# Attention: the first head pair begins its units after two groups' maxima, and takes the other groups' maxima inside its units

## The reference

```
s = einsum('bqhd,bkhd->bhqk', q_blk, k_all)
s = s + fq_blk.transpose(0, 2, 1)[..., None] - f_k[:, :, None, :]     # F = running sum of log forget values
s = where(kpos <= qpos, s, -inf)
p = softmax(s, axis=-1)
o = einsum('bhqk,bkhd->bqhd', p, v_all)
```

## Time and profile before

| | us |
|---|---|
| median of 3 runs | 3133.67 |
| the 3 runs | 3128.68, 3133.67, 3133.70 |
| the profiled execution | 3129.55 |
| its span, first to last instruction | 3128.0 |
| its mean granted PE clock | 0.945 of 2.4 GHz |
| attention: PE's first transpose to the first unit | 2004.04 to 2044.02 |
| attention: the 8 pairs' units | 2044.02 to about 2850 |

### The profile page before, as it was taken

One profiled execution on the slowest core, in us unless ns is written; L12 is line 12 of the kernel. 1 busy time (PEld: TensorE's weight loads), 2 busy tenths in 40 slices (PEclk: granted clock), 3 DMA queues, 4 the chain that ended last, 5 costly groups with the idle time before them and its releaser, 6 DMA issues. The chain is left out here.

```text
span 3128.0 us, 41449 instructions
## 1 busy us (share of the span) xinstructions
PE 2843.9 (91%) x15730; PEld 2033.8 (65%) x15730; DVE 1476.7 (47%) x3562; ACT 945.1 (30%) x1547; POOL 804.0 (26%) x460
## 2 busy tenths in 40 slices
PE   5589999997899996999969999789999999994999
PEld 2367777776677874788758777455555555552767
DVE  1542222211787646641157015566666666653343
ACT  0322222211555654220033112134444444433000
POOL 1220000000000002000011000268887888786000
PEclk7589999999899998999989999789999999997999
DMA  9532222212566435211151331333313431313764
GB/s 337 196 89 81 54 85 81 78 48 87 178 209 218 155 98 200 78 59 67 49 177 48 78 72 50 101 109 100 88 57 106 116 93 37 112 34 134 245 204 133
DMA packets 281927, 355.20 MB, mean 114 GB/s; under 512 B 40044, under 2 KB 172460, under 8 KB 281681
## 3 DMA queue, kind: packets, MB, share of 16 engines
q1 hardware_dynamic: 279364, 344.23, 34.9%
q0 software_dynamic: 2304, 8.39, 0.7%
q10 hardware_dynamic: 72, 0.07, 0.0%
HBM read 250.28 MB, written 102.10 MB: 113 GB/s over the span
## 5 line engine op out<-in xcount | busy, mean ns | idle before, releaser
L2341 POOL TENSOR_TENSOR at_p_sum<-at_p_sum,at_p 128x1024 f32<-128x1024 f32 (+3 forms) x264 | 521.9, 1977 | 84.5 <-ACT at_p L2187 61.6
L2187 ACT ACTIVATE at_p<-psum 128x1024 f32<-128x1024 f32 (+1 forms) x320 | 270.3, 895 | 383.8 <-PE psum L2014 376.7
L2238 DVE CUSTOM_DVE_ANT_0 psum<-psum,at_f_wide 128x512 f32<-128x512 f32 (+3 forms) x640 | 377.0, 631 | 0.0
L672 POOL TENSOR_TENSOR kv_h_lo<-kv_aux,kv_h_hi 128x512 fp32r<-128x512 f32 x16 | 24.1, 1507 | 1059.6 <-ACT kv_h_hi L649 1028.7
L2094 PE MATMUL psum<-at_p,at_v 128*64 128x512 f32 (+3 forms) x1280 | 270.5, 544 | 0.7 <-ACT at_p L2187 0.7
L768 PE MATMUL psum<-kv_w_hi,kv_h_hi 128*128 128x512 f32 x512 | 201.3, 393 | 13.0 <-DVE kv_w_lo L964 13.0
L768 PE MATMUL psum<-gla_w_hi,gla_h_hi 128*128 128x512 f32 x512 | 201.4, 393 | 2.7 <-DVE gla_w_lo L964 2.7
L769 PE MATMUL psum<-kv_w_lo,kv_h_hi 128*128 128x512 f32 x512 | 200.3, 391 | 0.0
L770 PE MATMUL psum<-kv_w_hi,kv_h_lo 128*128 128x512 f32 x512 | 200.2, 391 | 0.0
L769 PE MATMUL psum<-gla_w_lo,gla_h_hi 128*128 128x512 f32 x512 | 199.4, 390 | 0.0
L770 PE MATMUL psum<-gla_w_hi,gla_h_lo 128*128 128x512 f32 x512 | 199.3, 389 | 0.0
(11 more groups left out here) (425 smaller groups left out, 6196.3 us busy)
## 6 DMA issues: line engine op xcount, KB each, us to landing
mod_w<-in_ada_w SPq DMA_DIRECT2D x12, 2048.0 KB, 18.1
at_f_wide<-F SPq DMA_DIRECT2D x32, 512.0 KB, 5.0
at_page<-in_cache_k SPq DMA_DIRECT2D x32, 512.0 KB, 3.6
gla_w_raw<-in_gla_w_in SPq DMA_DIRECT2D x6, 2048.0 KB, 7.7
mod_w<-in_kv_ada_w SPq DMA_DIRECT2D x4, 2048.0 KB, 9.7
v_gla<-gla_stage SPq DMA_DIRECT2D x32, 256.0 KB, 2.0
sg_gla<-gla_stage SPq DMA_DIRECT2D x32, 256.0 KB, 2.0
gl_sg<-sg_gla SPq DMA_DIRECT2D x16, 512.0 KB, 3.9
```

The lines of the kernel that those rows point to most:

```text
L672: pool.tensor_tensor(part(h_lo, k, G), h_tmp[0], part(h_hi, k, G).bitcast(F32), ALU.subtract)\
L2187: act.activation(p_tile[e % PT][:, :, skip:NB], pair_of(bank_st[e % 2])[:, :, skip:NB], ACT.Exp)\
L2238: op = dve.tensor_tensor_reduce(pair_of(at(n))[:, a, 0:w], pair_of(at(n))[:, a, 0:w], f_wide[:, a, c * NB:c * NB + w], 1.0, -3.0e38, ALU.s ...
L2341: pool.tensor_tensor(p_sum[s][:, :, skip:NB], p_sum[s][:, :, skip:NB], p_tile[e % PT][:, :, skip:NB], ALU.add).then_inc(p_added, 1)
```

## The change

The prologue ends after group 1. Out of it go the transposes of group 3 (`turn` 3), the 12 maxima of group 2, its `m_max` and its `m_row`. These go into the first pair's units: the transposes to units 0 and 1, `m_row` of group 2 to unit 9, and the pair's list of maxima becomes 12 (group 2), 16 (group 3), 24 (next pair), 52 in 40 units. The twelve units of `two_maxima` carry two. In PE's order the second stands between the logits of e and those of e+1 (`max_unit(j, u, e, 1)`). Units on odd numbers keep one. Some odd jobs change their unit: `m_row` of group 3 goes from 17 to 21, the next pair's transposes move by up to three units, its `m_row` of group 0 from 23 to 25. SP loads the next pair's rows after the first pair's last transpose, no longer waits for a maximum ahead of the forget sums, and loads the wide forget sums at units 11, 13, 17 and 21 instead of 4, 8, 12 and 16. Later pairs keep their order.

```diff
@@ -1785,12 +1785,37 @@
     first_slots, n_max, FIRST = [], 0, 0
     for f in [("turn", 0, 0), ("turn", 0, 1), ("turn", 1, 0)] + ahead[0:2] + [("turn", 1, 1)] + ahead[2:4] + \
             [("m_max", 0, 0), ("turn", 2, 0)] + ahead[4:6] + [("m_row", 0, 0)] + ahead[6:8] + [("turn", 2, 1)] + ahead[8:12] + \
-            [("m_max", 1, 0), ("turn", 3, 0)] + ahead[12:15] + [("m_row", 1, 0)] + ahead[15:18] + [("turn", 3, 1)] + \
-            ahead[18:24] + [("m_max", 2, 0), ("m_row", 2, 0)]:
+            [("m_max", 1, 0), ("m_row", 1, 0)]:
         first_slots.append((OWN,) + f + ((n_max if f[0] == "max" else FIRST),))
         n_max += f[0] == "max"
         FIRST += f[0] in ("turn", "m_row")
-    start_slots, AT_START = slots_with(OWN, NEXT)
+    start_turns = {0: (OWN, "turn", 3, 0), 1: (OWN, "turn", 3, 1), 6: (OWN, "sum", 0, 0), 7: (OWN, "pick", 0, 0), 8: (OWN, "spread", 0, 0),
+                   9: (OWN, "m_row", 2, 0), 11: (NEXT, "turn", 0, 0), 12: (NEXT, "turn", 0, 1), 13: (NEXT, "turn", 1, 0),
+                   14: (OWN, "sum", 1, 0), 15: (OWN, "pick", 1, 0), 16: (OWN, "spread", 1, 0), 18: (NEXT, "turn", 1, 1),
+                   20: (NEXT, "turn", 2, 0), 21: (OWN, "m_row", 3, 0), 22: (NEXT, "turn", 2, 1), 25: (NEXT, "m_row", 0, 0),
+                   26: (OWN, "sum", 2, 0), 27: (OWN, "pick", 2, 0), 28: (OWN, "spread", 2, 0), 30: (NEXT, "m_row", 1, 0),
+                   32: (NEXT, "turn", 3, 0), 35: (NEXT, "turn", 3, 1)}
+    BEGUN = units_to(1)
+    two_maxima = (0, 2, 4, 6, 8, 10, 12, 22, 24, 26, 28, 30)
+
+    def first_pair_slots():
+
+        todo = [(OWN, f, BEGUN + n) for n, f in enumerate(ahead[BEGUN:] + last_maxima)] + [(NEXT, f, n) for n, f in enumerate(ahead)]
+        ends = {("max", R * G + R - 1, G) for G in range(NG)}
+        slots, n_turn = [[] for _ in range(UN)], 0
+        for e in range(UN):
+            for _ in range(1 + (e in two_maxima)):
+                who, f, n = todo.pop(0)
+                slots[e].append((who,) + f + (n,))
+                if f in ends:
+                    slots[e].append((who, "m_max", f[1] // R, 0, 0))
+            if e in start_turns:
+                slots[e].append(start_turns[e] + (n_turn,))
+                n_turn += 1
+        assert not todo
+        return slots, n_turn
+
+    start_slots, AT_START = first_pair_slots()
     mid_slots, EACH = slots_with(LAST, CARRIED, OWN, NEXT)
     end_slots, _ = slots_with(LAST, CARRIED, OWN)
     tail_slots = [(LAST,) + f[1:4] + (n,) for n, f in enumerate(f for f in turn_slots.values() if f[0] == LAST)]
@@ -1800,7 +1825,7 @@
     assert UN - 1 not in turn_slots
     page_at = (1, 10, 20, 31)
     score_at = (5, 7, 12, 14, 27, 29, 36, 38)
-    f_slots = (R, 2 * R, 3 * R, 4 * R)
+    first_f_slots, later_f_slots = (11, 13, 17, 21), (R, 2 * R, 3 * R, 4 * R)
     PT = 5
     with ExitStack() as st:
         sb = lambda n, s, d=F32: st.enter_context(nc.sbuf_tensor(f"at_{n}", s, d))
@@ -1956,16 +1981,18 @@
                     is_more = not is_last(j, u)
                     if is_more:
                         nxt = following(j, u)
-                        sp.wait_ge(turn_full, before(j, u))
+                        sp.wait_ge(turn_full, before(j, u) + 2 * is_first(j, u))
                         load_rows(*nxt)
-                        sp.wait_ge(max_full, UN * (2 * j + u) + AHEAD + 3)
                         if is_first(j, u):
                             sp.wait_ge(cleared, len(clears))
+                        else:
+                            sp.wait_ge(max_full, UN * (2 * j + u) + AHEAD + 3)
                         load_f(*nxt)
                         load_v(*nxt)
                         sp.wait_ge(page_done, PG * (2 * j + u) + 2)
                         load_q_sample(*nxt)
                     for e in range(UN):
+                        f_slots = first_f_slots if is_first(j, u) else later_f_slots
                         if is_more and e in f_slots:
                             sp.wait_ge(max_done, UN * (2 * j + u) + AHEAD + R * f_slots.index(e) + R + 1)
                             load_f_wide(*nxt, f_slots.index(e))
@@ -2107,15 +2134,14 @@
                     if kind == "spread":
                         spread_out(j, u, base, a, n)
 
-                def max_unit(j, u, e):
-
-                    for who, kind, t, c, n in slots_of(j, u)[e]:
-                        if kind == "max":
-                            at = whose(who, j, u)
-                            max_wait(*at, t, c, n)
-                            if c == t // R:
-                                masks(bank_max, t % R * P, g.hide_qk)
-                            maxima(*at, t, c)
+                def max_unit(j, u, e, nth):
+
+                    for who, kind, t, c, n in [f for f in slots_of(j, u)[e] if f[1] == "max"][nth:nth + 1]:
+                        at = whose(who, j, u)
+                        max_wait(*at, t, c, n)
+                        if c == t // R:
+                            masks(bank_max, t % R * P, g.hide_qk)
+                        maxima(*at, t, c)
 
                 def turn_unit(j, u, e):
 
@@ -2129,10 +2155,11 @@
                         G, i = exp_units[s]
                         if i >= R * G:
                             masks(bank_st[s % 2], (i - R * G) * P, g.hide_kq)
-                    max_unit(j, u, e)
+                    max_unit(j, u, e, 0)
                     logits(j, u, e)
+                    max_unit(j, u, e, 1)
                     logits(j, u, e + 1)
-                    max_unit(j, u, e + 1)
+                    max_unit(j, u, e + 1, 0)
                     turn_unit(j, u, e)
                     if e:
                         weigh_v(j, u, e - 2)
@@ -2157,7 +2184,7 @@
                         maxima(0, 0, a, b, first_max(n))
                     if kind == "m_row":
                         m_row(0, 0, 0, a, n, first_turn(n), 1)
-                pe.wait_ge(max_done, AHEAD + 1)
+                pe.wait_ge(max_done, BEGUN + 1)
                 pe.wait_ge(turn_used, FIRST + 1)
                 pe.wait_ge(cleared, CLEARED)
                 run_steps(step)
```

## The result

The median of 13 runs went from 3129.45 us (3125.79 to 3136.91) to **3139.49 us** (3136.43 to 3144.89). The ratio is **1.0034, 95% interval 1.0027 to 1.0042**: 10.6 us slower, 8.4 to 13.1. The profiled execution of the changed kernel took 3143.49 us, its span is 3141.9, its mean granted clock 0.945 as before.

What follows compares the result with a forecast made beforehand. DVE bounds the prologue, PE the units. Second maxima, `m_row` and store waits add 12.1 + 4.8 + 5.1 + 0.3 + 2.8 = 25.1 us, less 17.07 gained: 8.0 slower, 3141.7 from the median 3133.67; range 3134 to 3150.

Steps and rivals of the forecast that it cites:

- The prologue's gain: Ahead of the units: the first unit starts 1.56 us after group 1's `m_max`, at 2026.95 instead of 2044.02, 17.07 us gained.
- Doubles 0 and 2: First pair's start, at 1.2 GHz with round trips of 2.36: 2.9 and 2.2 us more, 5.1 together.
- Doubles 4 and 6: Wide doubles of the first pair: third maximum 4.12 us after the first instead of 2.18, 1.94 more each.
- Doubles 8, 10, 12: First pair: round trips add 2.06 us each in 8 and 10, 1.94 in 12; `m_row` 0.3, its store wait 1.4.
- Clock: I add nothing: First pair's units: the clock's rise comes no later than doubles 0 and 2, already costed at 1.2 GHz; nothing added.
- The stores: PE waits at units 12 and 24 for the row maxima's stores after `m_row`: 1.4 us each, 2.8 together.
- Doubles 22 to 30: Late in the first pair: about 1.2 us more each in 22, 24, 26, 30, and 2.14 in 28; store wait 1.4.
- Double 28: Wide double late in the first pair whose second maximum is masked, the mask 0.20 more: 2.14 us more.
- The later pairs and doubles 32 to 38: After the moved maxima: later pairs run the same order and stay as they are; no cost was given for these doubles.
- the second: Rival: an engine other than PE, POOL above all, ends the doubles, so waits are free; 9.4 us faster, 3124.3; chance 0.08.
- The third: Rival: the clock rises three doubles later or falls back among the waits; 3148.9 to 3153.7 us; chance 0.11.

Runs made afterwards that it cites:

- kernel 1: Changed kernel, but DVE reduces only the first 128 keys of each maximum in the twelve units with two maxima; ratio 0.9997 to the kernel before.
- kernel 4: Changed kernel with the twelve second maxima moved to odd units 1 to 13 and 23 to 31, between the two `weigh_v`; ratio 0.9997 to the kernel before.
- kernel 9: As kernel 4, but with long doubles chosen for the twelve second maxima (units 1 to 11, 15, 17, 19, 27, 29, 33); ratio 0.9993 to the kernel before.
- kernel 12: Kernel 9 with unit 11's second maximum moved to 35, `m_row` of group 3 at unit 20; 3124.89 us, ratio 0.9989 to the kernel before.
- kernel 7: Changed kernel with second and third maxima issued head by head, `m_row` of groups 2 and 3 earlier, transposes apart; ratio 1.0039 to the kernel before.

## Why the prediction was right, and where it was off

The forecast was slower by over 0.2%, by 8.0 us; the runs give 10.6, and the median of 3139.49 lies 2.2 below the 3141.7 named. That closeness is partly luck: the three runs shown had a median of 3133.67, the 13 runs of before 3129.45, and the sum was 2.6 too small. Between the two profiles, prologue and first pair came out at 12.0 us.

- **The prologue's gain**: 17.07 forecast, 17.09 measured. The step held: DVE's order up to group 1's `m_max`, then the same 1.56 (2027.76 to 2029.31).
- **Doubles 0 and 2**: 5.1 forecast; 3.03 and 1.98, together 5.0, measured (exponential to exponential). The agreement is luck: the parts named for double 0 add up to 7.9 with 1.0 for each transpose, not 8.1, and the two transposes took 2.98 on PE (2035.09 to 2038.07), with the uncosted wait of 1.41 at 2037.16 for their single buffer. The third maximum of double 0 was shorter, 0.47 for 0.7 (2034.62 to 2035.09), and not all of it ran at 1.2 GHz.
- **Doubles 4 and 6**: 1.94 each; measured 1.94 and 2.28. The round trip of 2.06 held to 0.01; the idle reads 0.64, not 0.80, since the row counts it from the end of the last matmul (0.40 long), where I had counted from the place of the next (0.23 on).
- **Doubles 8, 10, 12**: 7.8 forecast with `m_row` and its wait; 10.7 measured. **This is the step that was too small.** Two things were missing. "Clock: I add nothing" failed: it fell back at 2067.3 for 3.4 us, and a `weigh_v` took 3.57 instead of 1.94, 1.6 us. And the second single buffer, which transposes, `spread` and `m_row` share, was costed at nothing: 0.58 before `spread` at 2066.57, 0.6 before a transpose. Together 2.8 of the 2.9.
- **The stores**: 1.4 each, 2.8; measured 1.29 and 1.07, at units 12 and 24 as forecast.
- **Doubles 22 to 30**: 8.3 forecast with the store's wait; 9.4 measured. Double 22 took 2.95 more, 1.88 of it without the store's 1.07; doubles 24, 26 and 30 took 1.3 to 1.4, so my 1.2 for short masked maxima was a little low. Double 28 took 2.54 for 2.14, with 0.34 of waiting ahead of `spread`.
- **The later pairs and doubles 32 to 38** are as they were, as forecast.

Of the rivals, the second (POOL sets the pace, so the waits are free) is excluded by the result, and by kernel 1: with most of the waits gone the ratio fell from 1.0034 to 0.9997. The third is right in part: the clock rose where I had said (2046.8, 17.5 us after the first masks), but fell back once after that. What I had not thought of is a rise within 0.8 us of the first exponential. The changed kernel has it too (2033.2) and loses it again at 2036.6, while PE waits 1.41 us for the transposes' buffer; in kernels 4, 9 and 12, with the second maximum between the `weigh_v`, the clock rises there and stays.

## What to carry to other kernels

Price a step that is moved by the round trip of the buffer that it goes through: PE needs as much other work between two uses (here 2.06 us) or it idles for the rest. With the same twelve maxima between the `weigh_v`, and DVE's odd jobs moved along, the time fell by about 11 us (ratio 1.0034 to 0.9997). Choose the place by the length of each stretch, and look at every single buffer that the moved jobs share, not only at the one that the change names. A wait that vanishes in the profile is a gain only when the timed runs show it.

## What was not expected of the hardware

**The clock's falls do not follow the idle time.** Over a whole pair this cannot be read, since PE idles less while it has 1.2 GHz (not at all in the last two stretches of kernel 7 above). So I compare stretches at 2.4 GHz, one of kernel 7 up to its second fall and the first of kernel 4, in the view of busy time:

```profile
2069.76:2100.49 30.73, 29.37 (x212) 16.93 (x208) 19.80 (x74) 12.81 (x17) 23.85 (x11) 1.00 0.31 74
```

```profile
2031.76:2052.24 20.48, 15.92 (x126) 9.45 (x124) 14.70 (x53) 8.41 (x12) 12.35 (x7) 1.00 0.88 234
```

Kernel 7 fell after 30.73 us in which PE idled 1.36; kernel 4 idled 4.56 in 20.48 us and did not fall in the pair at all. The changed kernel fell at 2067.3 after 20.5 us in which PE was busy 15.22. All kernels with the second maximum between the logits have 5.6 us or more of the pair at 1.2 GHz, those with twelve between the `weigh_v` 2.1 or less. The Trainium skill ("TensorE: Matmul & The Clock Gate", section "A second HAM failure mode: psum-queue depth-cycling") puts such swings down to short idles between groups of matmuls; the changed kernel against kernel 4 agrees with it, kernel 7's stretch against kernel 4's does not. What decides was not separated.

**A phase that nobody touched has another length in other kernels**: the last phase took 281.8 to 287.6 us in these profiles, and DVE's waits for its loads of `out_sgT` 113.1 to 118.0. That the edits cause it is not shown.
